# Adding attention's distance biases as a rounded part and its rest, and normalising two head chunks at a time

## The reference, cut to what matters

```python
s = jnp.einsum("bqhcd,bkhcd->bhcqk", q_blk, k).astype(jnp.float32) * scale + bias[None, :, None]
s = jnp.where(rel >= 0, s, -jnp.inf)
p = jax.nn.softmax(s, axis=-1)
a = (p[:, :, 0] - lam * p[:, :, 1]).astype(v.dtype)
return jnp.einsum("bhqk,bkhe->bqhe", a, v)
...
o = rms_norm(o, subln_g) * (1.0 - lambda_init)
return o.reshape(bsz, seq, N_HEADS * V_HEAD_DIM) @ w_o
```

## Time and profile before

| | before |
|---|---|
| median of three runs | 1582.42 us (1580.14 to 1585.79) |
| the profiled execution: its own time, its span | 1582.96 us, 1581.2 us |
| TensorE busy | 1493.3 us, 94% of the span |
| VectorE busy | 1117.6 us, 71% |
| ScalarE busy | 754.8 us, 48% |
| granted TensorE clock, mean | 0.968 of full |
| share of TensorE in the chain that ended last | 79% |

### The profile page before, as it was taken

One profiled execution on the slowest core, in us unless ns is written; L12 is line 12 of the kernel. 1 busy time (PEld: TensorE's weight loads), 2 busy tenths in 40 slices (PEclk: granted clock), 3 DMA queues, 4 the chain that ended last, 5 costly groups with the idle time before them and its releaser, 6 DMA issues.

```text
span 1581.2 us, 31078 instructions
## 1 busy us (share of the span) xinstructions
PE 1493.3 (94%) x11554; PEld 1408.4 (89%) x11554; DVE 1117.6 (71%) x1726; ACT 754.8 (48%) x1280; POOL 224.8 (14%) x237
## 2 busy tenths in 40 slices
PE   3999999999999999999999888989999999999997
PEld 2998799999997789999888877779999998899997
DVE  6888889987896678873686775267775365677743
ACT  3553655553446655564266511244444455644452
POOL 0000213321000113330000100011331000133310
PEclk8899999999999999999999978799999999999999
DMA  8544436689683325565332300034566443356661
GB/s 332 180 180 152 173 127 220 239 323 352 237 299 117 112 88 187 186 212 187 133 107 80 108 1 1 8 118 129 186 184 215 143 160 107 107 172 186 193 209 63
DMA packets 68135, 257.59 MB, mean 163 GB/s; under 512 B 7512, under 2 KB 9696, under 8 KB 67680
## 3 DMA queue, kind: packets, MB, share of 16 engines
q1 hardware_dynamic: 68064, 256.64, 48.3%
HBM read 255.55 MB, written 1.06 MB: 162 GB/s over the span
## 4 chain that ended last, share of the span: by engine, by line
PE 79%; DVE 13%; ACT 3%; DMA 2%; issue 2%; SPq 0%; ACTq 0%; DVEq 0%
PE ps L546 21%; PE ps L548 21%; PE ps L547 21%; PE ps L515 4%; DVE inv L1457 2%; DVE lo L1426 1%; DMA modraw<-in_wmod 1%; DVE modraw L1432 1%; PE ps L507 1%; DVE Y L1465 1%; PE ps L574 1%; PE ps L651 1%; PE ps L797 1%; DVE X L1470 1%; PE ps L564 1%
## 5 line engine op out<-in xcount | busy, mean ns | idle before, releaser
L546 PE MATMUL ps<-OH,lo 128*128 128x256 f32 x2176 | 628.1, 289 | 23.2 <-DVE lo L1426 5.8
L1426 DVE TENSOR_TENSOR lo<-raw,hi 128x1024 fp32r<-128x1024 f32 (+1 forms) x350 | 474.1, 1371 | 207.3 <-ACT hi L1003 206.8
L547 PE MATMUL ps<-OL,hi 128*128 128x256 f32 x2176 | 615.4, 283 | 0.0
L548 PE MATMUL ps<-OH,hi 128*128 128x256 f32 x2176 | 614.9, 283 | 0.0
L546 PEld LDWEIGHTS ps<-OH,lo 128*128 128x128 f32 x2176 | 412.7, 190 | 38.2 <-issue 11.5
L547 PEld LDWEIGHTS ps<-OL,hi 128*128 128x128 f32 x2176 | 415.8, 191 | 0.9
L548 PEld LDWEIGHTS ps<-OH,hi 128*128 128x128 f32 x2176 | 412.8, 190 | 0.0
L1003 ACT ACTIVATE hi<-raw 128x1024 fp32r<-128x1024 f32 (+1 forms) x350 | 379.9, 1110 | 14.7 <-PE ps L548 12.2
L546 PE MATMUL ps<-GH,lo 128*128 128x256 f32 x704 | 197.5, 281 | 0.0
L547 PE MATMUL ps<-GL,hi 128*128 128x256 f32 x704 | 197.5, 281 | 0.0
L548 PE MATMUL ps<-GH,hi 128*128 128x256 f32 x704 | 197.5, 281 | 0.0
(11 more groups left out here) (324 smaller groups left out, 1745.8 us busy)
## 6 DMA issues: line engine op xcount, KB each, us to landing
raw<-in_w SPq DMA_DIRECT2D x288, 512.0 KB, 3.6
raw<-in_w SPq DMA_DIRECT2D x64, 704.0 KB, 5.2
modraw<-in_wmod SPq DMA_DIRECT2D x85, 512.0 KB, 5.2
modlate<-in_wmod SPq DMA_DIRECT2D x6, 512.0 KB, 5.0
modlast<-in_wmod SPq DMA_DIRECT2D x5, 512.0 KB, 5.3
l<-in_lora_in SPq DMA_DIRECT2D x1, 1536.0 KB, 6.6
l<-in_lora_out SPq DMA_DIRECT2D x1, 1536.0 KB, 10.0
X<-in_xin SPq DMA_DIRECT2D x1, 1024.0 KB, 6.5
```

The costliest lines, as they stand in the source:

```text
L546: pe.matmul(bank[:, 0:T], lo[:, r, w], oh[:, k0 + k], start=first, stop=False)
L547: pe.matmul(bank[:, 0:T], hi[:, r, w], ol[:, k0 + k], start=False, stop=False)
L548: ins = pe.matmul(bank[:, 0:T], hi[:, r, w], oh[:, k0 + k], start=False, stop=final)
L1426: dve.tensor_tensor(lo[:, s, 0:kt * P], raw[:, s, 0:kt * P], hi[:, s, 0:kt * P].bitcast(F32), ALU.subtract).then_inc(lo_made, 1)
```

## The change

- The biases are two tiles now. `bias_hi` is the reversed, negated bias rounded to F32R by ScalarE, behind the copy-out of att_q's unit 6. `bias_lo` is the rest that the rounding left, made by VectorE behind the last unit's `lo`, where `bias` was made. ScalarE also rounds the identity into `ident_r`, behind the copy-out of unit 5. A product of each part by the rounded identity gives the part back.
- `scores(n)` adds each of the two parts with an F32R matmul, so four F32R matmuls stand where two float32 matmuls were. TensorE starts the scores when all three tiles are made.
- ScalarE's part of att_q, a hardware loop before, is written out.
- The head norm goes by pairs of chunks. TensorE spreads two chunks into one bank (three banks, 5 to 7) and does one `keep_busy` matmul behind each pair; VectorE and ScalarE handle 512 columns in one instruction.

```diff
-        bias = at(11, "bias", [P, HEADS, T])
+        bias_hi = at(11, "bias_hi", [P, HEADS, T], F32R)
+        bias_lo = at(0, "bias_lo", [P, HEADS, T], F32R)
+        ident_r = at(3, "ident_r", [P, P], F32R, plus=4096)
...
-                for c in range(2):
-                    ins = pe.matmul(PS[2 * (n % 2) + c][:, 0:nk], ident, bias[:, h, T - nk:T], start=False, stop=True)
+                for part, last in ((bias_hi, False), (bias_lo, True)):
+                    for c in range(2):
+                        ins = pe.matmul(PS[2 * (n % 2) + c][:, 0:nk], ident_r[:], part[:, h, T - nk:T], start=False, stop=last)
                 ins.then_inc(S("att_scores"), 1)
 
-            pe.wait_ge(S("att_scaled"), 1)
+            pe.wait_ge(S("att_scaled"), 3)
...
             for c in range(HEADS):
-                wait(pe, S("o_normed"), c - 2)
-                pe.matmul(PS[1 + c % 3][:, 0:T], ident[0:HEADS, c:c + 1].to_broadcast([HEADS, P]), inv[0:HEADS, 0],
-                          start=True, stop=True).then_inc(S("o_spread"), 1)
+                wait(pe, S("o_normed"), c // 2 - 2)
+                pe.matmul(PS[5 + c // 2 % 3][:, c % 2 * T:(c % 2 + 1) * T], ident[0:HEADS, c:c + 1].to_broadcast([HEADS, P]),
+                          inv[0:HEADS, 0], start=True, stop=True).then_inc(S("o_spread"), 1)
+                if c % 2:
+                    keep_busy(1, 1)
...
-            layer("att_q", copy_out(Q, scale=-HEAD_DIM ** -0.5))
+            queries_out = copy_out(Q, scale=-HEAD_DIM ** -0.5)
+
+            def queries_and_biases(i, r, u):
+                queries_out(i, r, u)
+                if 4 * i + r == COUNT["att_q"] - 3:
+                    act.activation(ident_r[:], ident, ACT.Copy).then_inc(S("att_scaled"), 1)
+                if 4 * i + r == COUNT["att_q"] - 2:
+                    act.wait_ge(S("bias_landed"), 16)
+                    act.activation(bias_hi[:], biasrev[:, :, ::-1], ACT.Copy, scale=-1.0).then_inc(S("att_scaled"), 1)
+            layer("att_q", queries_and_biases, peel_first=True)
...
-            for c in range(DC):
-                act.wait_ge(S("o_normed"), c + 1)
-                act.activation(OH[:, c], O[:, c], ACT.Copy).then_inc(S("oh_ready"), 1)
+            for p in range(DC // 2):
+                act.wait_ge(S("o_normed"), p + 1)
+                act.activation(OH[:, 2 * p:2 * p + 2], O[:, 2 * p:2 * p + 2], ACT.Copy).then_inc(S("oh_ready"), 2)
...
                     dve.wait_ge(S("bias_landed"), 16)
-                    dve.tensor_scalar(bias[:], biasrev[:, :, ::-1], -1.0, None, ALU.mult).then_inc(S("att_scaled"), 1)
+                    dve.wait_ge(S("att_scaled"), 2)
+                    dve.wait_ge(mod_done, LAST_MODS)
+                    stt(out=bias_lo[:], in0=biasrev[:, :, ::-1], scalar=-1.0, in1=bias_hi[:].bitcast(F32), op0=ALU.mult,
+                        op1=ALU.subtract).then_inc(S("att_scaled"), 1)
...
-            for c in range(DC + 2):
-                if c < DC:
-                    dve.wait_ge(S("o_spread"), c + 1)
-                    stt(out=O[:, c], in0=O[:, c], scalar=small[:, 0:1], in1=PS[1 + c % 3][:, 0:T], op0=ALU.mult, op1=ALU.mult
+            for p in range(DC // 2 + 1):
+                if p < DC // 2:
+                    dve.wait_ge(S("o_spread"), 2 * p + 2)
+                    y = O[:, 2 * p:2 * p + 2].rearrange("p c t -> p (c t)")
+                    stt(out=y, in0=y, scalar=small[:, 0:1], in1=PS[5 + p % 3][:, :], op0=ALU.mult, op1=ALU.mult
                         ).then_inc(S("o_normed"), 1)
-                if c >= 2:
-                    low_part(O, OH, OL, c - 2)
+                if p:
+                    last = slice(2 * p - 2, 2 * p)
+                    oh_count[0] += 2
+                    dve.wait_ge(S("oh_ready"), oh_count[0])
+                    dve.tensor_tensor(OL[:, last], O[:, last], OH[:, last].bitcast(F32), ALU.subtract
+                                      ).then_inc(operand_ready, 2)
```

## The result

The changed kernel takes 1588.58 us (median of 20 runs, 1583.83 to 1592.6), the kernel before 1582.33 us (20 runs, 1578.99 to 1592.74). The ratio is 1.0033 with a 95% interval of 1.0021 to 1.0045. The range given ended at 1584.0, and the chance given to slower by over 0.3% was 0.07.

A forecast was written before the change was run, and what follows sets the result against it. TensorE was taken as the bound (in the chain for 79% of the span), with the 256-column bias add wholly on the path. Attention -2.35 and head norm -0.2 took 1582.4 to 1579.8 us, range 1576.3 to 1584.0.

The forecast's parts named there:

- The cheaper bias add: Attention: four F32R matmuls of 256 columns take 0.50 us less a head; -2.9 us at full clock, -1.9 us at 1.2 GHz.
- The later start: Start of attention: scores wait for bias_lo and begin at 485.4 instead of 483.64, +1.75 us.
- The low clock at the scores: First scores of attention all come behind the clock's fall, at half clock: +0.7 us.
- The price of the narrow adds: Attention's 128-column bias adds: four F32R matmuls take 0.4 to 1.0 us against 0.71; 0 on the path.
- The head norm: Head norm to att_out's unit 0: 24 records cost +1.4 us, the clock holding gives -1.6 us; together -0.2 us.
- Rival 1: Head norm: the clock falls all the same, 8-row matmuls counting for little; 1581.5 us, chance 0.24.
- Rival 4: Attention stays at 1.2 GHz, heads about 5.3 us, +6.7 over six heads instead of -2.9; 1589 us, chance 0.06.
- Rival 3: Attention: narrow F32R matmuls as dear as float32, or ScalarE the bound; 1580.6 to 1581.4 us, chance 0.12.
- Rivals 2 and 5: First: clock back earlier in attention, 1579.0 us, chance 0.12. Second: the bias parts save nothing, 1584.6 us, chance 0.04.

The follow-up runs named there:

- bias_only: The changed kernel with the old head norm, so the new biases alone: 1586.32 us, ratio 1.001 against the kernel before.
- after_again: The changed kernel timed and profiled once more, with no edit: 1588.65 us, ratio 1.0028 against the kernel before.
- norm_kb_full: norm_only with spreads of 128 rows instead of 8, busy matmuls kept: 1584.87 us, ratio 1.0005 against the kernel before.
- norm_only: The kernel before with the new pairwise head norm alone, old biases kept: 1588.35 us, ratio 1.0031 against the kernel before.
- bias_fill: bias_only with six busy matmuls of 256 columns in TensorE's wait ahead of the scores: 1581.18 us, ratio 0.9986 against the kernel before.
- before_fill: The kernel before with two busy matmuls of 256 columns in TensorE's wait for the biases: 1582.27 us, ratio 0.9986 (0.997 to 1.0003).
- norm_nokb: norm_only without the busy matmul behind each pair of spreads: 1582.47 us, ratio 0.9989 against the kernel before.
- norm_full: norm_nokb with spreads of 128 rows instead of 8: 1586.65 us, ratio 1.0013 against the kernel before.

## Why the prediction was wrong, point by point

- **The cheaper bias add** was right in kind, a little too large: 0.38 less in the chain instead of 0.50. The four matmuls go at 0.145 us apart and not at 0.118, and the sum took 1.13 us for the old add, from the timeline, where the chain has 1.07. Heads are 3.79 us apart where 3.69 was forecast. Attention at equal low time gained 3.1 to 3.6 us.
- **The later start** was right: 2.28 us for `bias_lo` (2.21), 1.91 for `bias_hi` (1.90), +1.6 us (1.75).
- **The low clock at the scores** was mis-sized. The prediction let it end where it had ended before, at 492.1, and charged +0.7. It was 10.2 us long in three profiles and 17.1 in one, and at some 0.3 us for each low microsecond that takes about 2 us more than the old start's average of 5.1. With it the biases come out at nothing: bias_only 1.001. The price of the narrow adds was also taken too low there: 1.04 us for four of 128 columns at the low clock, nearly as much as for the 256 columns (1.15), and more than the 0.71 of the old add, which ran at the full clock. Attention was to give 4.1 us without the start; it gave 2.6 in the first pair of profiles and 0.4 in after_again against before.
- **The head norm** is the step that failed: "I take it that the clock holds: -1.6 us." The clock fell 4.9 us after the reciprocal's end, as before (5.0), but TensorE was now still in the spreads, and it stayed low for twice as long; TensorE did the last pair at half speed. From the reciprocal's end to the first copy-out 8.8 us were forecast (5.7 + 3.1) and 12.97 measured (7.91 + 5.06). Two terms were wrong. The busy matmuls cost more than their pitch, 1.68 a pair instead of 1.43, since 8-row and 128-row matmuls follow each other more slowly than equals (1.30 in norm_kb_full): 1.0 us. And a third of full-row matmuls didn't hold the clock: 1.2 us in the spreads and 2.0 in unit 0. norm_kb_full shows that full rows in the spreads hold it, and there the stage takes 8.86 us, the -0.2 forecast. It is +3.95 for the stage (9.0 to 12.95) where -0.2 stood.
- **The rivals.** Rival 1, the clock falling all the same, was the right mechanism, but only the old loss was put back (1581.5); that the stretch of 8-row matmuls had been made longer, with the fall now inside it, wasn't priced. Rival 4, the low clock staying into the heads, came in part: in after_again the clock was low until 500.5, the 8 us beyond 492 from which that rival was to decide. Its 1589 us lies beside the measured 1588.6 by luck: it put the loss into attention, at 5.3 us a head, and heads went at 3.79 while the head norm lost the time. Rival 3 came in part: a head lets 0.39 us through instead of 0.49, and `aT` no longer waits, but the chain of a head doesn't lead through `aT`. Rivals 2 and 5 fell.
- **The range**: its lower end should read 1576.5 by its own terms (1579.0 less 2.5), not 1576.3; nothing hangs on it.

Stage by stage, after against before: +1.6 start, -2.6 attention (with its 10.2 low), +3.95 norm, together +3.0 in the two profiles and +5.4 for after_again against before. The medians are 6.3 us apart in the first comparison and 4.5 in the last job; where the part of the 6.3 came from that the first two profiles don't show is open.

The whole runs add a split between the two parts. Take (1 - mean granted clock) x time of each run as its clock loss. In the last job it is 53.1 us for the 35 runs of before and 59.2 for the 12 of after_again, 6.1 more, while the mean time is 4.5 more (1589.0 against 1584.5). bias_only has 4.5 more of it than its job's runs of before and takes 1.5 more on the mean; norm_only has 1.1 more and takes 4.6 more. So the biases' part shows as clock, which eats what they save, and most of the head norm's loss against the kernel before is not clock but the busy matmuls' own time, as the 6.7 us of pairs say too. (The forecast had priced 1.4 us of that time, so what it missed is mostly clock.) The measure can't be subtracted one for one: among the runs of before a microsecond of it goes with 0.7 to 0.9 us of time.

## What to carry to other kernels

Price a busy matmul like any other on the path, and look at what stands around it: put between matmuls of 8 rows it cost 0.6 us apiece and the clock fell anyway, while in these profiles giving the neighbours full rows, for no extra columns, held it. Where an engine's wait ahead of a stage grows by even 1.6 us, ask what that does to the clock of the stage behind it; busy matmuls in the wait took 3.2 us off attention in bias_fill, as much as the cheaper arithmetic gave (3.1 to 3.6); what two of them gain alone, in before_fill (36.2 us instead of 38.5), one profile and an interval over 1 don't settle. And a gain of a few microseconds can't be read from whole runs whose clock varies by more: compare stages in the profile, and the granted clock of the runs.

## What was not expected of the hardware

- 128-row and 8-row float32 matmuls in turns: 1.68 us for four 8-row records and two 128-row ones, 1.30 us for the six with equal rows, at a granted clock of 1.00 in both.
- Sixteen spread records of 8 rows (3.70 us, norm_nokb) and of 128 rows (3.63 us, norm_full), all of 256 columns: the granted clock was 0.50 from 1.0 us behind the first and stayed at 1.00 behind the second.
- The clock at 1.2 GHz for 17.1 us, through stretches in which TensorE's rows show it busy for 4.00 of 4.00 us (after_again). The Trainium skill, "TensorE: Matmul & The Clock Gate", Part 1, says that sustained activity releases the throttle; in the changed kernel the clock rose 3.8 us after att_out's first matmul, and at attention's start, where float32, 64-row and F32R matmuls are mixed, after 3.4 to 17.1 us at 1.2 GHz (3.4 in norm_only, 17.1 in after_again).
- Four F32R matmuls of 128 columns took 1.04 us at the low clock in the chain, four of 256 columns 1.15: the width counts for little there.
